# The first stage of a decoder-layer kernel, cut into halves

## The reference, cut to what matters

```python
shift, scale, gate = split(silu(c) @ w_ada + b_ada, 3)
h = rmsnorm(x, g_pre) * (1 + scale) + shift
hc, bc, cc, gc, q, k, v, ga = split(h @ w_in, 8)       # 512 channels each
ya = rmsnorm(bc * conv3(cc * hc), g_conv) * silu(gc)
# stick breaking: z = q.k/8 + b_sb; log_keep = log_sigmoid(-z) where s < t
# a = exp(log_sigmoid(z) + later log_keep);  o = a @ v
yb = rmsnorm(o, g_attn) * silu(ga)
y = x + gate * rmsnorm(concat(ya, yb) @ w_out, g_post)
```

## Time and profile before

| | us |
|---|---|
| median of 3 runs | 875.83 |
| the three runs | 872.63, 875.83, 875.88 |
| the profiled execution's own time | 872.5 |
| its span, first to last instruction | 870.7 |

### The profile page before, as it was taken

One profiled execution on the slowest core, in us unless ns is written; L12 is line 12 of the kernel. 1 busy time (PEld: TensorE's weight loads), 2 busy tenths in 40 slices (PEclk: granted clock), 3 DMA queues, 4 the chain that ended last, 5 costly groups with the idle time before them and its releaser, 6 DMA issues.

```text
span 870.7 us, 15500 instructions
## 1 busy us (share of the span) xinstructions
PE 825.4 (95%) x4267; PEld 488.4 (56%) x4267; DVE 526.9 (61%) x691; ACT 348.9 (40%) x682; POOL 376.9 (43%) x186
## 2 busy tenths in 40 slices
PE   0899989999999999999999999999999999899996
PEld 0455756555667565565765655658555555344442
DVE  2554678676584767737857768287686774223334
ACT  6311057574112575811136666211565741111222
POOL 0006782653677355525865455268446430100000
PEclk9989999999999999999999999999999999999998
DMA  8997685576788866657888675687986757373101
GB/s 320 331 309 254 219 268 168 170 226 207 234 253 270 276 208 215 222 172 252 270 271 261 223 244 177 200 256 252 282 249 212 238 185 302 106 236 100 71 24 51
DMA packets 129221, 191.25 MB, mean 220 GB/s; under 512 B 9817, under 2 KB 50822, under 8 KB 129121
## 3 DMA queue, kind: packets, MB, share of 16 engines
q1 hardware_dynamic: 97920, 174.38, 60.9%
q10 hardware_dynamic: 31200, 15.73, 6.4%
HBM read 181.58 MB, written 8.51 MB: 218 GB/s over the span
## 4 chain that ended last, share of the span: by engine, by line
PE 88%; DVE 3%; issue 2%; SPq 2%; DMA 2%; ACT 1%; POOL 1%; POOLq 0%; DVEq 0%; ACTq 0%
PE ps L1144 83%; PE ps L1300 4%; DMA pages<-in_page_table_dram 1%; PE ps L1185 1%; SPq L319 1%; POOL prod L539 1%; DMA hT<-in_w_out_dram 1%; DVE xy L851 1%; DVE ps L1024 0%; DMA ring<-in_cache_v_dram 0%; PE ps L1327 0%; SPq L359 0%; SPq L351 0%; DVE zc L1030 0%; ACT gcb L572 0%
## 5 line engine op out<-in xcount | busy, mean ns | idle before, releaser
L1144 PE MATMUL ps<-hT,wsl 128*128 128x344 f32 x1344 | 425.3, 458 | 3.5 <-issue 3.5
L539 POOL TENSOR_TENSOR prod<-ring,qb 128x1024 f32<-128x1024 f32 x128 | 313.2, 2470 | 220.3 <-DMA ring<-in_cache_k_dram 93.9
L1144 PEld LDWEIGHTS ps<-hT,wsl 128*128 128x128 f32 x1344 | 241.6, 190 | 156.7 <-issue 43.0
L1000 DVE TENSOR_REDUCE zd<-prod 128x16 f32<-128x1024 f32 x128 | 154.1, 1213 | 37.1 <-POOL prod L539 35.9
L1010 DVE TENSOR_SCALAR zc<-ps,bsb 128x512 f32<-128x512 f32 (+3 forms) x96 | 55.5, 613 | 70.3 <-PE ps L1144 68.9
L1144 PE MATMUL ps<-ring,apad 128*8 128x512 f32 (+1 forms) x608 | 82.9, 626 | 2.5 <-DMA ring<-in_cache_v_dram 2.2
L572 ACT ACTIVATE av<-ps 128x512 f32<-128x512 f32 (+3 forms) x96 | 46.7, 487 | 86.2 <-PE ps L1300 85.4
L1144 PE MATMUL ps<-hT,xy 128*128 128x512 f32 x160 | 72.1, 594 | 0.5 <-DMA hT<-in_w_out_dram 0.5
L1024 DVE TENSOR_TENSOR_SCAN ps<-rise,ps 128x512 f32<-128x512 f32 (+3 forms) x64 | 65.6, 1025 | 9.8 <-ACT ps L572 8.7
L1144 PEld LDWEIGHTS ps<-wsl,hT 128*128 128x128 f32 (+1 forms) x576 | 63.5, 181 | 6.2 <-ACT vN L572 2.6
L1144 PE MATMUL ps<-wsl,hT 128*128 128x128 f32 (+1 forms) x576 | 66.5, 275 | 0.0
(11 more groups left out here) (210 smaller groups left out, 662.6 us busy)
## 6 DMA issues: line engine op xcount, KB each, us to landing
ring<-in_cache_k_dram SPq DMA_DIRECT2D x256, 256.0 KB, 3.0
ring<-in_cache_v_dram SPq DMA_DIRECT2D x256, 256.0 KB, 3.0
wsl<-in_w_in_dram ACTq DMA_DIRECT2D x30, 512.0 KB, 5.7
ring<-in_w_ada_dram SPq DMA_DIRECT2D x6, 2048.0 KB, 11.3
xy<-in_x_prompt_dram SPq DMA_DIRECT2D x2, 2048.0 KB, 10.4
out_dram<-oT SPq DMA_DIRECT2D x8, 512.0 KB, 4.0
ring<-in_x_prompt_dram SPq DMA_DIRECT2D x8, 512.0 KB, 6.5
hT<-in_w_out_dram SPq DMA_DIRECT2D x5, 512.0 KB, 5.6
```

The costliest lines, as they stand in the source:

```text
L539: pool.tensor_tensor(prod[:, p % 2].rearrange("p (j c) -> p j c", j=2), kring[:, p % 4], qb[:, p // 16].unsqueeze(1).to_broadcast([P, 2, H ...
L1000: v.tensor_reduce(zd[:, t // 16, :, r:r + 2], prod[:, t % 2].rearrange("p (j h d) -> p h j d", j=2, h=NH), AX_X, ALU.add)\
L1144: return nc.tensor.matmul(out, l, r, start=start, stop=stop, skip_group_check=True)
```

## The change

The first stage goes by halves, in four ways. (1) SP loads the first half of x, the nine small transfers, the second half, slabs 0 and 2 of `w_ada` (shift and scale of channels 0 to 511), the Q and K weights, then slabs 1 and 3, and the rest. (2) Squares, means, scaling and turns go by halves of x; turns are ordered by half, and `ada(0)` stands between the halves. (3) The modulation goes by slab, and DVE applies channels 0 to 511 first. (4) PE does k 0 to 3 of all six Q and K chunks (`project_lo`, in six PSUM banks) before the other half of the modulation is there; the first pass's slots 0 to 5 do only k 4 to 7. Beside that, the first pass's page pairs stand at slots 5 to 31 and not at 0 to 31, `query_rows` is in slot 1, the gate's steps are in slots 3, 4, 7 and 8, and the first row's decode steps come later.

```diff
-ADA_AT = (6, 14)
+TURNS = [(k, 0, "dve" if k < 4 else "act") for k in range(KT)] + [(k, 1, "act" if k % 2 else "dve") for k in range(KT)]
+ADA_COLS = (0, 2, 1, 3)
+HK = KT // 2
+H_AT = (0, HK, 2 * HK + 1)
+H_STEP = 3 * HK + 1
...
-def pairs_at(slot):
+def pairs_at(slot, first):
+    if first:
+        ahead = [(), (), (), (), (), (0, 1), (2, 3, 4), (5, 6, 7), (8, 9), (10, 11), (12, 13), (14, 15)]
+        if slot < 12:
+            return ahead[slot]
+        late = [s for s in range(12, SLOTS) if s % 2 or s % 4 == 2 or s == 12]
...
+def decode_at(first):
+    return (12, 13, 14, 15, 18) if first else (8, 9, 10, 12, 14)
...  (DVE, first stage)
+            v.wait_ge(ssq, 4)
+            v.tensor_scalar(ss[:, 0:4], ss[:, 0:4], 1.0 / D, EPS, ALU.mult, ALU.add).then_inc(var_ready, 1)
+            v.wait_ge(rstd_ready, 1)
+            scale_tiles(0, 4)
+            for i in range(2):
+                turned(i)
             v.wait_ge(ssq, TT + 1)
...
+            for i in range(2, KT):
+                turned(i)
+            v.wait_ge(rstd_ready, 3)
+            scale_tiles(4, TT)
...
+            for i in range(2):
+                ks = slice(HK * i, HK * (i + 1))
+                up = slice(KT + HK * i, KT + HK * (i + 1))
+                v.wait_ge(mod_ps, i + 1)
...
+                for c in range(3):
...
+                    for k in range(HK * i, HK * (i + 1)):
+                        v.tensor_scalar(hT[:, k, cols], hT[:, k, cols], mods[:, KT + k, 0:1], mods[:, k, 0:1],
+                                        ALU.mult, ALU.add).then_inc(h_ready, 1)
...  (DVE, first pass)
-                    if first and t in (0, 5):
-                        gates(t // 5)
+                    if first and t in (3, 8):
+                        gates(t // 8)
...  (PE, first stage)
+            def project_lo(m):
+                part, chunk = (Q_, m) if m < 3 else (K_, m - 3)
+                if chunk == 0:
+                    pe.wait_ge(w_full[part % 2], 16)
+                for k in range(HK):
+                    pe.wait_ge(h_ready, H_AT[chunk] + k + 1)
+                    mm(ps[:, pj_bank(m, True), 0:CH], wsl[:, part % 2, k, :], hT[:, k, CH * chunk:CH * (chunk + 1)],
+                       k == 0, False)
+            turns(0)
             ada(0)
-            ada(1)
+            turns(1)
...
+            modulation(0)
+            ada(1)
+            modulation(1).then_inc(mod_ps, 1)
+            for m in range(3):
+                project_lo(m)
+            ada(2)
+            for m in range(3, 6):
+                project_lo(m)
+            modulation(2)
+            ada(3)
+            modulation(3).then_inc(mod_ps, 1)
...  (PE, first pass)
                 for t in range(8):
+                    ks = range(HK, KT) if first else range(KT)
...
                     if first and t == 0:
+                        pe.wait_ge(h_ready, H_STEP + H_AT[2])
+                        pe.wait_ge(par_copied, 2)
+                        strips(DB, lambda k: hT[:, k, SEQ:NTP], 4).then_inc(qs_ps, 1)
+                    if first and t == 1:
                         query_rows()
...
-                    if first and t in (1, 5):
-                        gate_strips(t // 5)
-                    if first and t in (2, 6):
-                        gate_sums(t // 6)
+                    if first and t in (3, 7):
+                        gate_strips(t // 7)
+                    if first and t == 4:
+                        gate_sums(0)
...
+                    if first and t == 8:
+                        gate_sums(1)
-                    if t == 12:
+                    if t == decode_at(first)[3]:
                         cumulate(0)
```

More of the change, by code:

```diff
@@ L401, in body @@
                         load_q(g, 1)
+                    if first and t == 6:
                         load_ada(7, ada_v[5])
@@ L531, in body @@
                 for t in range(SLOTS):
-                    for p in pairs_at(t):
+                    for p in pairs_at(t, first):
                         if p % 16 == 0:
@@ new lines, in _, with turned @@
+            act.wait_ge(x_in[0], 16)
+            for t in range(4):
+                square_tile(t, t)
+            act.wait_ge(x_in[1], 16)
+            for t in range(4, TT):
+                square_tile(t, t)
+            act.wait_ge(small_in, 16 * N_SMALL)
+            act.wait_ge(ssq, TT - 1)
+            run(hcb[0:NB, 0:D], xs, ACT.Square, ssq, accum_out=ss[0:NB, TT:TT + 1])
+            def turned(half_):
+                for i, (k, hf, owner) in enumerate(TURNS):
+                    if owner == "act" and hf == half_:
+                        act.wait_ge(xT_full, i + 1)
+                        run(hT[:, k, HALF * hf:HALF * (hf + 1)], ps[:, i % 4, :], ACT.Copy, xT_act)
@@ L858, in _ @@
                 .then_inc(xT_sdve, 1)
[L861 to L866, removed]
@@ L867, in _ @@
-            v.wait_ge(xT_act, KT)
-            v.wait_ge(xT_sdve, 1)
[L869 to L875, removed]
+            v.wait_ge(xT_act, sum(owner == "act" for _, _, owner in TURNS))
@@ L942, in body @@
                     if t > 0:
-                        for p in pairs_at(t - 1):
+                        for p in pairs_at(t - 1, first):
                             reduce_pair(g, p)
@@ L1170, in ada @@
             def ada(n):
-                if n >= 2:
-                    pe.wait_ge(ada_copied, n - 1)
-                strips(PJB + n % 2, lambda k: cT[:, k, :], n).then_inc(ada_ps, 1)
-            ada(0)
-            ada(1)
[L1178 to L1185, removed]
-                                               xy[:, 4 * (n % 2) + j, P * (n // 2):P * (n // 2 + 1)], ident[:, :])
-                last.then_inc(xT_full, 1)
+                if n == 3:
+                    pe.wait_ge(ada_copied, 3)
@@ new lines, in ada, with turns @@
+                strips((PJB, PJB + 1, DB, DB)[n], lambda k: cT[:, k, :], n).then_inc(ada_ps, 1)
+            def turns(half_):
+                for i, (k, hf, owner) in enumerate(TURNS):
+                    if hf != half_:
+                        continue
+                    if k == 0:
+                        pe.wait_ge(x_scaled, 4 if hf == 0 else TT + 1)
+                    if i >= 4:
+                        before = TURNS[i - 4][2]
+                        pe.wait_ge(xT_act if before == "act" else xT_dve, sum(o == before for _, _, o in TURNS[:i - 3]))
+                    for j in range(4):
+                        last = nc.tensor.transpose(ps[:, i % 4, P * j:P * (j + 1)],
+                                                   xy[:, 4 * hf + j, P * k:P * (k + 1)], ident[:, :])
+                    last.then_inc(xT_full, 1)
@@ new lines, in modulation @@
+            def modulation(n):
+                pe.wait_ge(ada_copied, n + 1)
+                for k in range(4 * ADA_COLS[n], 4 * ADA_COLS[n] + 4):
+                    last = mm(ps[:, MB, 256 + 9 * k:265 + 9 * k], ada_cols(P * k, P), e32[:, 0:9], True, True)
+                return last
+            def project_lo(m):
[6 more added lines that the diff above has]
+                       k == 0, False)
@@ L1221, in project @@
                 def project(m, part, chunk, ks=range(KT)):
-                    if first and part == Q_:
-                        pe.wait_ge(h_ready, 1 + KT * (chunk + 1))
                     if ks[0] == 0:
@@ L1230, in project @@
                     for k in ks:
-                        last = mm(ps[:, PJB + m % 2, 0:CH], wsl[:, part % 2, k, :], hT[:, k, CH * chunk:CH * (chunk + 1)],
+                        if first and part == Q_:
+                            pe.wait_ge(h_ready, H_STEP + H_AT[chunk] + k - HK + 1)
+                        last = mm(ps[:, pj_bank(m, first), 0:CH], wsl[:, part % 2, k, :], hT[:, k, CH * chunk:CH * (chunk + 1)],
                                   k == 0, k == KT - 1)
```

132 lines of the change are left out of this document (73 added, 59 removed).

## The result

| | before | after |
|---|---|---|
| median us | 874.74 (872.48 to 875.88, 11 runs) | 877.52 (876.05 to 882.21, 11 runs) |
| ratio, 95% interval | | 1.005 (1.0033 to 1.0066) |
| profiled execution: span | 870.7 | 880.5 |

The changed kernel is slower by 0.5%, some 4 us (the interval is 2.9 to 5.8 us; the means differ by 4.1, the medians by 2.8). Forecast was +3.7 us, a profiled time of 876.2 and a median of 878. The profiled execution after is the slowest of the eleven, 882.2, and the trace shows what of the 9.8 us between the spans belongs to the change: at the end of the first pass it is 5.0 late, and the rest came after that point, where the program is the same.

What follows compares the result with a forecast made beforehand. The prediction took PE as the bound, with 88% of the chain of waits. It summed -7.1 us up to slot 8 and +10.8 from there to +3.7: profiled time 876.2, median 878, range 869 to 885.

Steps and rivals of the forecast that it cites:

- The way to slot 8: First stage and slots 0 to 7: PE starts slot 8 at 104.3, not 111.38, 7.1 us earlier (bounds 4.5 and 9.5).
- The term of 1.8: First stage on PE: one fall to the half-rate clock costs 1.8 us (bounds 0 and 3.6).
- The first cut: First-stage stretch of short products and waits on PE, forecast at 35.2 to 38.5, 3.3 us; clock fall there left open.
- the second: Second such stretch on PE, forecast at 57.6 to 60.9, just before slot 0, 3.3 us; clock fall left open.
- The pairs: Slots 8 to 13: PE waits behind page pairs bound to POOL's 2.36 us products; cost 10.8 us (bounds 8 and 13).
- T: Start of slot 8 on PE, forecast at 104.3 us against 111.38 before; later times are counted from it.
- the clock rival: Clock falls at both first-stage cuts and again in slot 8's wait: +6.6 us, 879 by the profile; chance 0.14.
- the hole before pair 7: POOL idles 10 us or more before slot 8's pair 7, waiting until PE's scores let DVE go on.
- The sum: Whole kernel: 7.1 us gained before slot 8, 10.8 lost from there, +3.7 us; profiled time 876.2, median 878.
- the 2.8 owed: Part of the 7.1 us gain before slot 8 that is only deferred: gate_sums(1), 2.76 us, moves to slot 8.
- The faster rival: Slots 8 to 13 keep their old waits, so the catch-up stays hidden: -4.3 us, about 868 by profile; chance 0.18.

Runs made afterwards that it cites:

- experiment 1: Changed kernel with first-pass page pairs moved to earlier slots, meant to put ten ahead of slot 8; ratio 1.003 to the kernel before, 1.8 us less than the changed kernel.
- experiment 2: Changed kernel with DVE's gates(1) in slot 8 put ahead of the three reductions; ratio 1.0082 to the kernel before, 2.8 us more than the changed kernel.
- experiment 3: Changed kernel with POOL's product in the first pass's first 16 pairs cut to one page of two; ratio 0.9993 to the kernel before.
- experiment 5: Changed kernel's first stage with pairs and decode steps in the old slots, gates(1) kept in slot 8; ratio 1.0167 to the kernel before.
- experiment 6: Changed kernel with first-pass pairs and decode steps placed by POOL's pace, gate's second half back ahead of slot 8; ratio 0.996 to the kernel before.
- experiment 7: Changed kernel plus six unread 128x256 PE products at each of the first stage's two cuts; ratio 1.0016 to the kernel before.
- experiment 8: Changed kernel with both POOL-paced slots and six unread PE products at each first-stage cut; ratio 0.9921 to the kernel before, median 867.83 us.
- experiment 4: Kernel before, with its own first stage but the changed kernel's slots for pairs, gate and decode steps; ratio 1.0104 to the kernel before, 9 us more.

## Why the prediction was right

**The way to slot 8: right, by errors that cancel.** Turns at 18.66 (18.0 said, where its terms give 17.8), `project_lo` at 38.73 (38.5), slot 0 at 62.47 (62.65 with one fall of the clock), slot 8 at 105.14 (104.3). Beneath: the second half of x came at 17.14 and not 15.8, 2.4 later than before where 1 was said. Of this 0.5 is the first half's own delay (10.17 for 9.66); most of the rest is in the window of 9 to 11 us, where 98 GB/s were moved and not the 276 that the forecast took. `ada(0)` made this good, at the full clock in 1.92 and not 3.64. The power of four columns, taken as 1.0 between 0.53 and 1.66, took 1.02.

```profile
9.00:11.00 2.00, 0.89 (x8) 0.92 (x8) 0.97 (x1) 0.83 (x1) 0.00 (x0) 1.00 0.34 98
```

**The clock: one fall taken, two happened.** The term of 1.8 (bounds 0 to 3.6) was too small in this trace. The first cut took 8.87 for 7.2, the second 3.90 for 2.45. Over six traces of kernels with these cuts and no filler (the changed one and experiments 1, 2, 3, 5, 6) the first fell in four and stayed full in experiments 2 and 3 (7.18), and the second fell in five and stayed full in experiment 5 (2.58, with a wait of 0.33 for the strips where the prediction had 0.7). The same instructions, shifted by under 1 us, get either. A trace lost 1.7 to 3.5 us by it, and what decides was not found. It is not shown to be what spreads the changed kernel's runs over 6 us: with the cuts filled they spread over 5.4.

The Trainium skill's rule (TensorE: Matmul & The Clock Gate, "HAM oscillation — how this bites in real kernels") that work cut up by waits keeps falling back to the slow clock, left undecided in the prediction, is borne out here in the main. The clock fell at 9 of 12 cuts over these six traces, and at none of the four that experiments 7 and 8 filled.

**The pairs: right in mechanism, and nearly in size.** The gate's wait 3.87 (4.05 said), then none, 1.61, 1.00, 1.75 (1.4, 2.0, 1.1, 1.8 said); `turn(4)` at T+30.65 (T+30.2). The wait missing in slot 9 is the slow clock: PE's 2.45 of projection took 4.51 there, and `turn(0)` came at T+13.3 and not 12.0. This was the clock rival's point, and as it said against itself, the slack of slots 9 to 12 took most of it up. Behind 145 us PE waits for nothing more in the pass, as was said. What failed is the hole before pair 7: 10 us on POOL said, 5.3 found (DVE's was 10.1). The first product came at 79.51 and not 77.7, and POOL waited 3.2 more for pair 5's page, which SP issues behind the last slab. It changed no cost, since products 5 and 6 were done by T, but it is what made experiment 1 fail.

**The sum.** -7.1 + 10.8 = +3.7; measured in the trace to the end of the pass +5.0 (219.24 against 214.27 for the same projection), by the ratio +4.4. The missing 1.3 is 0.8 at slot 8 and 0.5 behind it: T came 6.2 earlier and not 7.1. Experiment 4 parts the two terms, taken in this order: 9.1 for the slots where 8.0 was said, and then 4.7 for the first stage where 4.3 was (7.1 less the 2.8 owed). On the old slots the second term has the other sign (experiment 5); the forecast did not claim otherwise.

**Behind the pass.** From `turn(6)` to the end of the span it is 731.5 before, 736.9 after, and 734.4, 733.9, 734.3 and 733.5 in experiments 1, 2, 3 and 7, which run the same instructions there up to the moved `cumulate(0)`. Both profiled executions compared here are extremes of that spread. The profiled time after was said to be 876.2 and was 882.2, which is a miss. The ratio's 4.4 stands for all runs, but its interval is 2.9 to 5.8, so that it lies so near to 3.7 is in part luck.

The rows say where the trace after lost its last 4.8: 1.2 between the end of the first pass and the last stage (`ps<-hT,xy` at 737.38 for 731.19), and 3.5 in the 34 us behind (771.47 for 761.75). There PE waited for output weights, and the products behind the wait ran at a granted clock of 0.60 on average (742 to 746).

```profile
733.52 1.12 PE L1144 MATMUL ps<-hT,xy 128*128 128x512 f32 x2 [0.45 <-DMA hT<-in_w_out_dram]
...
741.66 1.12 PE L1209 MATMUL ps<-hT,xy 128*128 128x512 f32 x2 [2.40 <-DMA hT<-in_w_out_dram]
```

The first line is of before, the second of after. In the traces of all eight experiments this wait is between none and 1.06, so the 2.40 is not the change's as far as they show; what made it long was not tried.

The faster rival failed on the point named: PE waits behind the pairs because `log_weights` does. It would have been near the truth for the paced slots of experiment 6 (-3.5 where it says -4.3), in which the same catch-up is hidden.

## What to carry to other kernels

When a stage is made shorter, look at what starts by its end: here the strips that make the pages' queries moved behind the early halves (66.30, before 51.64), the first product came 9 us later while PE reached slot 8 6 us earlier, and the gain turned into a debt in an ordered queue. Place the steps of a slower engine by its own pace (first result, time of one, free slots) and never let it stand idle before a stretch in which it is the limit. Cutting TensorE work into parts with short waits between can cost more than the waits: here 1.7 to 3.5 us a trace in slower clock, and six products at each cut that nothing reads were cheaper (3.0 us gained).

## What the runs showed of the hardware

A DVE instruction with two SBUF inputs is held up by a running POOL product, until about 0.55 us after that product's end. DVE's 8x512 product of `gates` (line 953) takes 0.68 alone, and beside POOL it took 0.96 and 1.72, 1.74 and 1.02 in the changed kernel, 3.32 to 3.35 in experiments 1, 4 and 7 and 3.92 in experiment 5. Wherever POOL stood still it took 0.68 (six times over the ten traces; so in the second half of the gate in experiments 2, 6 and 8). The first and the last line here are of experiment 5, alone and beside POOL; between them stands line 958, also with two SBUF inputs, 0.69 alone and 2.77 here, where POOL's first product had begun at 82.90:

```profile
81.11 0.68 DVE L953 TENSOR_TENSOR rows<-rows,gp 8x512 f32<-8x512 f32 x1
...
83.08 2.77 DVE L958 TENSOR_TENSOR gp<-gp,ub 128x512 f32<-128x512 f32 x1
...
123.70 3.92 DVE L953 TENSOR_TENSOR rows<-rows,gp 8x512 f32<-8x512 f32 x1
```

In the trace of the kernel before, POOL's products ran until 102.05, and the 1.72 of the earlier trace rows ended at 102.60:

```profile
78.45 23.60 POOL L539 TENSOR_TENSOR prod<-ring,qb 128x1024 f32<-128x1024 f32 x10 [3.53 <-DVE zd L1000]
```

In experiment 5 the 3.92 ended at 127.62, 0.55 after a product that ended at 127.07; it had begun beside an earlier product, and passed two changes from one POOL instruction to the next. In the changed kernel the step ran from 112.00 to 113.02, across the change from one product to the next, and that next product took longer than 2.35:

```profile
112.44 2.81 POOL L560 TENSOR_TENSOR prod<-ring,qb 128x1024 f32<-128x1024 f32 x1
```

The reductions (one input) took 1.22 beside POOL as without, and so did line 951, with one input in PSUM: 0.67 beside POOL (111.30 in the changed kernel) and 0.68 without. The forecast's price for line 953, 1.72, was too long here by 0.7. What it took from the Trainium skill (GPSIMD Engine Reference, "Specifications"), that the two engines share interfaces to SBUF for DVE instructions with two SBUF inputs, agrees with these rows. The price is what is left of POOL's running instruction, and in the four longest cases the next as well: 0.3 to 3.2 us. It was seen in every trace, not tried by itself.
